# Which engine makes the sums of weights for a seven-product matmul, and in which slots the convolution taps stand

## The reference, cut to what matters

```python
u = rms_norm(h, norm_mix[l])
proj = u @ w_in[l]                        # 2048 -> 5408 columns
conv_val, conv_gate, rwkv_cols = ...      # 1024, 1024 and 3360 columns
# convolution branch
c = conv_val * sigmoid(conv_gate)
c = depthwise_conv(c, dw, width 31, causal) + bias
y_conv = silu(layer_norm(c))
# RWKV branch, 16 heads of 64, state S of 64 x 64 per head
S = S * w + (S a) b^T + v k^T ;  y = S r
h = h + concat(y_conv, y_rwkv) @ w_out[l]
```

## Time and profile before

| | |
|---|---|
| median of 3 runs (lowest to highest) | 3846.77 us (3846.37 to 3851.57) |
| the profiled execution | 3847.7 us, its span 3845.7 us |
| mean granted TensorE clock of the profiled execution | 0.972 |
| TensorE busy over the span | 3487.7 us (91%) |
| VectorE busy | 1504.8 us (39%) |
| GpSimd busy | 631.6 us (16%) |

### The profile page before, as it was taken

One profiled execution on the slowest core, in us unless ns is written; L12 is line 12 of the kernel. 1 busy time (PEld: TensorE's weight loads), 2 busy tenths in 40 slices (PEclk: granted clock), 3 DMA queues, 4 the chain that ended last, 5 costly groups with the idle time before them and its releaser, 6 DMA issues. The chain is left out here.

```text
span 3845.7 us, 51326 instructions
## 1 busy us (share of the span) xinstructions
PE 3487.7 (91%) x21663; PEld 2374.3 (62%) x21663; DVE 1504.8 (39%) x2464; ACT 567.9 (15%) x1088; POOL 631.6 (16%) x496
## 2 busy tenths in 40 slices
PE   8999999997899887777777768999999999999999
PEld 5887777776545433222232227754488888888888
DVE  4567677787411200000000004664133355454442
ACT  2222222222201100000000004201100010331000
POOL 1423332222000000000000000032000000465511
PEclk9999999998899899999999989999999999999999
DMA  3321121113051699999999987334433322222432
GB/s 112 84 56 49 45 59 52 48 41 138 2 188 45 257 421 422 422 422 422 420 421 420 417 337 186 91 90 110 103 110 110 115 88 88 77 82 99 157 113 77
DMA packets 321259, 672.80 MB, mean 175 GB/s; under 512 B 43228, under 2 KB 227974, under 8 KB 267685
## 3 DMA queue, kind: packets, MB, share of 16 engines
q1 hardware_dynamic: 312293, 639.50, 45.8%
q0 software_dynamic: 8768, 30.42, 2.2%
HBM read 639.58 MB, written 47.05 MB: 179 GB/s over the span
## 5 line engine op out<-in xcount | busy, mean ns | idle before, releaser
L2652 PE MATMUL stream_bank<-whole_big 128*128 128x256 f32 x3584 | 783.4, 380 | 0.7 <-DVE whole_big L2703 0.4
L2652 PEld LDWEIGHTS stream_bank<-whole_big 128*128 128x128 f32 x3584 | 679.0, 190 | 97.7 <-issue 4.5
L2126 PE MATMUL experts_run_bank<-whole_big 128*64 128x512 f32 x2048 | 485.9, 621 | 174.7 <-DMA whole_big<-in_expert_w_gate 103.5
L310 PE MATMUL first_bank<-whole_big 128*128 128x256 f32 x2240 | 542.1, 391 | 0.0
L310 PEld LDWEIGHTS first_bank<-whole_big 128*128 128x128 f32 x2240 | 416.4, 192 | 91.1 <-issue 30.1
L2126 PEld LDWEIGHTS experts_run_bank<-whole_big 128*64 128x64 f32 x2048 | 169.3, 142 | 490.6 <-issue 490.5
L2703 DVE TENSOR_TENSOR whole_big<-stream_bank,whole_big 128x256 f32<-128x256 f32 x292 | 119.2, 421 | 429.3 <-PE stream_bank L2652 429.3
L2557 PE MATMUL stream_bank<-whole_big 128*128 128x512 f32 x640 | 278.8, 594 | 0.0
L2191 DVE TENSOR_TENSOR whole_big<-whole_big,experts_run_bank 128x512 f32<-128x512 f32 x16 | 11.0, 687 | 650.4 <-PE experts_run_bank L2126 650.4
L2146 PE MATMUL experts_run_bank<-whole_big 128*64 128x512 f32 x1024 | 230.0, 596 | 35.1 <-DMA whole_big<-in_expert_w_down 22.7
L2557 PEld LDWEIGHTS stream_bank<-whole_big 128*128 128x128 f32 x640 | 120.2, 190 | 145.5 <-issue 145.0
(11 more groups left out here) (476 smaller groups left out, 3757.2 us busy)
## 6 DMA issues: line engine op xcount, KB each, us to landing
whole_big<-in_expert_w_gate SPq DMA_DIRECT2D x128, 1024.0 KB, 27.5
whole_big<-in_expert_w_up SPq DMA_DIRECT2D x128, 1024.0 KB, 29.7
whole_big<-in_expert_w_down SPq DMA_DIRECT2D x128, 1024.0 KB, 26.7
whole_big<-in_w_in SPq DMA_DIRECT2D x110, 1024.0 KB, 5.9
whole_big<-in_w_out SPq DMA_DIRECT2D x16, 1024.0 KB, 7.6
whole_big<-in_w_out SPq DMA_DIRECT2D x8, 2048.0 KB, 12.8
gates_two<-whole_big SPq DMA_DIRECT2D x40, 256.0 KB, 7.9
whole_big<-gates_two POOLq DMA_DIRECT2D x40, 256.0 KB, 3.0
```

Of the source, the lines that this page charges most:

```text
L310: mm = pe.matmul(self.place(m), weights[:, k, :], left[:, k, :], start=(k == 0), stop=(k == 7))
L2126: mm = pe.matmul(bank[self.half(h), :], self.x_T[:, PARTS * q + k, self.half(h)], self.ring[slot][:, k, :], start=(q == 0 and k == 0), sto ...
L2652: mm = pe.matmul(self.place[m % 3], weights[:, k, :], left[:, k, :], start=(k == 0), stop=(k == self.k - 1))
```

## The change

Three edits.

1. The sums of weights inside the pairs go from GpSimd's queue to VectorE's, into `rest`, behind the `take`s and ahead of the taps of the slot; and they come two slots after that in which product 5 or 6 was finished, where GpSimd had them one slot after. The sums of groups 0 to 5, before the pairs, stay with GpSimd.
2. `t1_to_3` gets one more wait, for the four sums of the group before.
3. Pairs 0 to 4 have no taps in S1 to S6, and eight in Y in place of two. Pair 5 has none in S1 to S6, eight in Y, and one more in L0, L1, L2b, L4 and M and one fewer in F. Pair 6 moves five taps from S1 to S4 and S6 into H, M and F. The number of taps of a pair stays what it is.

```diff
-CONV_SHARE = (0, 3, 0, 1, 2, 2, 1, 2, 1, 1, 2, 1, 1, 4, 1, 2, 1, 1, 1, 1, 1, 1, 2)
-CONV_TWO_THIRDS = (0, 4, 1, 2, 3, 2, 2, 3, 2, 2, 2, 2, 2, 4, 2, 3, 2, 2, 1, 2, 2, 1, 2)
-CONV_LAST = (0, 3, 0, 2, 2, 2, 2, 3, 2, 0, 0, 2, 2, 4, 3, 4, 2, 2, 2, 2, 2, 3, 4)
+CONV_SHARE = (0, 3, 0, 1, 2, 2, 1, 2, 1, 1, 2, 1, 1, 4, 1, 2, 0, 0, 0, 0, 0, 0, 8)
+CONV_TWO_THIRDS = (0, 4, 1, 3, 3, 3, 2, 3, 3, 2, 2, 3, 2, 4, 3, 2, 0, 0, 0, 0, 0, 0, 8)
+CONV_LAST = (0, 3, 0, 2, 2, 2, 2, 3, 2, 0, 0, 2, 2, 6, 4, 6, 1, 1, 1, 1, 2, 2, 4)
@@ t1_to_3
             eng.wait_ge(self.product, 2)
+        if n:
+            eng.wait_ge(self.summed, 4 * n)
         eng.tensor_tensor(t1, b12, b11, ALU.subtract).then_inc(self.summed, 1)
@@ vector: pair(j)
+                    def sums(slot):
+                        for m in finished_by(j, slot - 2):
+                            n, i = divmod(m, 7)
+                            if i == 5 and FIRST_GROUPS < n + 1 < GROUPS_ONE:
+                                dense.t1_to_3(dve, n + 1)
+                            elif i == 6 and FIRST_GROUPS < n + 1 < GROUPS_ONE:
+                                dense.t4(dve, n + 1)
+
                     def rest(name):
                         i = SLOTS_ONE.index(name)
                         if i:
                             for m in finished(j, i - 1):
                                 take(m)
+                            sums(i)
                         n = TAPS_OF_PAIR[j][i]
@@
                     if j:
                         for m in finished(j - 1, len(SLOTS_ONE) - 1):
                             take(m)
+                        sums(0)
                     rest("A1")
@@ gpsimd: slot_work(j, slot)
-                    for m in finished_by(j, slot - 1):
-                        n, i = divmod(m, 7)
-                        if i == 5 and n + 1 < GROUPS_ONE:
-                            dense.t1_to_3(pool, n + 1)
-                        elif i == 6 and n + 1 < GROUPS_ONE:
-                            dense.t4(pool, n + 1)
```

## The result

The changed kernel takes 3818.2 us (median of 4 runs, 3817.5 to 3820.4) beside 3849.2 us for the kernel before on the same occasions: 0.9918 of it, 95% interval 0.9905 to 0.9931, or 31 us less. Its profiled execution has a span of 3816.1 us, 29.6 us less than before. The forecast was 36 us less.

What follows compares the result with a forecast made beforehand. TensorE was taken to bound the pairs, through waits for VectorE and low clock: 54 us recoverable, 17 staying, 0.7 added, so about -36 us from 3846.8 to 3811 us. Range 3796 to 3838 us.

Steps and rivals of the forecast that it cites:

- The bound: In the pairs TensorE sets the end; its waits for VectorE, 38.4 us, and low clock, 15, make about 54 recoverable.
- The hold-up by GpSimd: While GpSimd sums, VectorE's instructions with two SBUF inputs last longer: 121 us in all; VectorE to become lighter by about 55.
- The price of a sum: On VectorE one sum takes 1.17 us, three 3.5, a group 4.65; 14 groups add 65 us.
- The lumps: Sums standing in VectorE's queue in S slots and levels make TensorE wait anew, 13 us in sum.
- The rule of 3.5 us between two advances: In S slots, VectorE may do 3.5 us of other work between two state advances before TensorE waits.
- The clock: TensorE's time at 1.2 GHz after waits costs 15 us; two stretches, in pairs 1 and 4, stay at 2 us each.
- the eight taps in Y: Six more taps, 4.0 us, hidden in VectorE's gap ahead of the next pair's first mask.
- pair 6's taps: In pair 6's S chain, where VectorE sets the pace, the last advance comes one tap later: +0.7 us.
- Carried to the end: Behind the pairs, the experts' stretch has DMA engines busy 0.99 of the time, so the pairs' gain arrives in full.
- The even exchange: Rival: VectorE's own sums take the time it gets back, leaving only the taps' move; 3841 to 3847 us, chance 0.07.
- VectorE's queue holds the chains: Slower rival: sums delay identity or advance; up to 3857 to 3879 us, deciding from 3.9 us uncovered a group; chance 0.10.
- More lumps bite: Rival: room wrong by 1.5 us at each of 14 places, or low clock; 21 us less gained, 3832; chance 0.15.

Runs made afterwards that it cites:

- the kernel without sums: Changed kernel without the 56 sums inside the pairs, the semaphore raised in their place and products using what stands in the buffers: 3795.0 us, 0.9864 of before.
- the two loads: Changed kernel plus, at the old sums' places on GpSimd, twelve SBUF-reading multiplications per group: 3862.7 us; or 56 memsets per group that only write: 3814.1 us.
- The runs with the levels and with the state placed: Changed kernel, better slots only for sums in levels and pair starts: 3807.4 us; only for those in M and S, three taps to Y: 3810.4 us.
- the last run: Kernel with all sums in better slots, plus pair 6's taps moved from H, F and the S slots to Y: 3790.3 us, 0.9843 of before.
- the run with the sums alone: Changed kernel with the taps back in their old slots, so only the sums moved to VectorE: 3823.5 us, 0.9940 of before.

## Why the prediction came out

**The bound.** Right. TensorE sets the end in the pairs and the waits for VectorE are what can be won: the kernel without sums, with 2.8 us of these waits left up to 860 us, takes 52 us less than the kernel before on its occasion (3847.4 to 3795.0), and the forecast had called 54 recoverable from pair 0 to the start of pair 6. The agreement is closer than the estimate deserves, since the cost of the low clock was a guess between 0 and 21.

**The hold-up by GpSimd.** Right in kind, and shown by the two loads; too large in size. Of the 121 us in which VectorE was said to stand inside instructions, the three groups gave back 35 + 52 + 14 = 101: an addition of 128x512 stays at 799 ns, not the 0.68 us taken for it, because GpSimd's masks and gated tiles still read SBUF (three additions at 843.02 take 3.70 us beside two masks from 842.49 on). VectorE's busy time over the span falls by 37 us (1504.8 to 1468.0), not 55.

**The price of a sum.** 3.53 us for three against 3.5; 72 us of busy time for all, against 65. Standing alone in a row each is 1.22 us, which makes 68; the rest is what some of them lose beside GpSimd's masks and gated tiles.

**The lumps.** This is the term that was too small: 13 us of new waits were forecast and 19.9 came. The rule of 3.5 us between two advances held: 4.03 us against 4.1 in pair 1, 1.20 against 1.4 in pair 4, 0.59 against 0.8 in pair 0. Pair 4's second wait, 2.58 against 2.8, is near too, but the sum as written (1.3 + 3.4 with room of 3.5) would give 1.2: directly behind a wait only one period of 2.19 us is room, and the advances of 715.67 and 720.50 are 4.83 us apart, 2.6 more. In the levels 2.31 against 2.4 and 0.93 against 0.8. Four places were missed by 7.7 us together, and the 0.6 us of pair 1's t4 did not come. Three of the four share one mistake, in the steps that count the work at the start of pair 6 "from the first mask to the identity", say of M that it has "less work than the contention took", and of L3 that it has "the room": a part of VectorE's work does not start where the last gap ended but behind a further wait for TensorE, and sums behind that wait have no slack of what lies ahead of it. At the start of pair 6:

```profile
851.47 0.69 DVE L1203 TENSOR_TENSOR whole_big<-first_bank,whole_big 128x512 f32<-128x512 f32 x1 [1.53 <-PE first_bank L753]
852.52 0.69 DVE L1371 SCALAR_TENSOR_TENSOR whole_big<-first_bank,whole_big 128x512 f32<-128x512 f32 x1 [0.35 <-PE first_bank L788]
...
856.55 2.30 DVE L328 TENSOR_TENSOR whole_big<-whole_big 128x1024 f32<-128x1024 f32 x1
```

VectorE stands still twice, 1.53 and 0.35 us, before the second mask and the centring, and the token shift and the sums come only then: wait 2.10 us, forecast none. About half of it is that. The other half, 1.1 us, is contention again, for the first sum takes 2.30 us where one alone takes 1.22, beside this mask:

```profile
856.25 1.52 POOL L1611 TENSOR_TENSOR whole_big<-whole_big 128x512 f32<-128x512 f32 x1 [10.28 <-PE first_bank L769]
```

(The forecast's own figures for this place, 8 + 4.65 + 3.4 = 16.1 us of work in 15.5 of room, did not give "none" either; only the fourth sum, which stands behind the identity, takes 1.15 off.) Pair 0's L3 (1.43, none) has the same mistake: the last wait ends at 249.82, and token shift and sums lie behind it. So has pair 5's M (2.28, none), where it ends at 810.06, but there the sums make only half: the kernel without sums still waits 1.16 us at this matmul, for the token shift and the two taps of F that stand between two advances, which the forecast did not count. The fourth, pair 2's L0b (2.14 against 0.3), is contention that stays: two taps behind the sums take

```profile
445.51 3.44 DVE L1303 SCALAR_TENSOR_TENSOR whole_big<-whole_big 128x512 f32<-128x512 f32 x2
```

where two take 1.4 alone, beside a mask and a gated tile on GpSimd. The runs with the levels and with the state placed show all four to be places and not a limit: each wait whose sums were moved went, or fell to what the kernel without sums has, or less where taps had moved too.

**The clock.** Time at 1.2 GHz stays in the two pairs that were named, 15 us of it, where two stretches that cost 2 us each had been taken. The forecast had the clock's cost fall from 15 to 4 us, by 11, and that can be read off. From 211 us to the last wait at the start of pair 6 TensorE does the same work in both kernels:

```profile
211.00:890.30 679.30, 640.07 (x7473) 502.85 (x7471) 510.43 (x621) 170.02 (x300) 204.94 (x107) 0.97 0.18 50
211.00:861.85 650.85, 630.99 (x7473) 496.45 (x7471) 472.41 (x676) 170.60 (x300) 62.36 (x51) 0.99 0.19 52
```

The first row is of the kernel before, the second of the changed one. 28.5 us are won here; 9.1 of them are busy time, the same instructions at a higher clock, and 19.4 are idle time. Over the whole span busy time falls by 10.7 us (3487.7 to 3477.0). So the clock's term came out, in one execution each, and the shortfall of some 6 us against the forecast is that of the new waits.

**The added wait, the eight taps in Y, pair 6's taps.** No wait of VectorE for a load or product appears, and none at the start of pair 3 beyond 0.32 us. Pair 6's S chain was to lose 0.7 us; its waits for L1441 and its first advance are 8.7 + 3.0 us where 10.2 + 1.2 stood, 0.3 more. That the taps cost a little there and gain when they go on to Y is what the last run shows. In the signs that the forecast named, the largest wait stood in pair 1 and none over 0.32 us at the starts of pairs 3 and 5; the one at the start of pair 6 was a miss.

**Carried to the end.** The span gained 29.6 us, and the experts' stretch is as it was: 0.99 of the DMA engines' time in a window of 990 us that begins 30 us earlier,

```profile
1280.00:2270.00 990.00, 761.88 (x3379) 288.61 (x3377) 71.67 (x110) 38.22 (x64) 37.63 (x62) 0.96 0.99 410
```

**The rivals.** The even exchange is out by the run with the sums alone. "VectorE's queue holds the chains" named the right mechanism for what is left, about 21 us, and its deciding point was not reached. "More lumps bite" had the direction of the miss, by 7 us and not 21.

## What to carry to other kernels

When work moves to an engine that stands in a chain, ask for its place before its sum: the same 56 instructions cost some 21 us two slots behind their due time and nothing measurable in slots that end in a wait anyway. For each lump find the last wait of that engine before it and the next instruction that another engine needs from it; only the time between these two counts as room, and idle time before that wait does not. And where two engines hold each other up, the mean duration of an instruction beside its shortest says how much is to be got back.

## What the hardware showed beyond that

GpSimd's reads in short pieces held VectorE up less than the long ones, and still cost a lot of time. Twelve reads of 0.99 us a group added 52 us to VectorE's busy time, where the old four of 2.6 us had cost it 101 us in three groups of instructions; yet that kernel is 44 us slower than the one without them. It also has the sums in VectorE's own queue, which the old one had not, so the comparison with the old kernel (1.0034) doesn't tell what splitting alone would do.

Whether a wait lowers TensorE's clock is not told by its length. In the changed kernel the 32 matmuls behind the wait of 2.31 us in pair 1 took 1.73 us, and those behind the wait of 2.14 us in pair 2 the usual 1.15. With the sums alone moved, the same two places had the same waits and it was the other way round:

```profile
347.08 1.15 PE L780 MATMUL first_bank<-whole_big 64*64 64x64 f32 x32 [2.31 <-DVE whole_big L1203]
445.82 1.98 PE L780 MATMUL first_bank<-whole_big 64*64 64x64 f32 x32 [2.15 <-DVE whole_big L1203]
```

What else decides is open.
